# A bidirectional attention and mLSTM layer on 8 cores: the softmax denominators made by one 512-column product, their reciprocal taken over 512 columns in four pieces

## What is computed

```
def one_block(qi):
    s = jnp.einsum('bqkgd,bskd->bkgqs', qi, k) * scale
    p = jax.nn.softmax(s, axis=-1)
    return jnp.einsum('bkgqs,bskd->bqkgd', p, v)
...
attn_out = blocked_gqa_attention(aq, ak, av).astype(x.dtype) * jax.nn.silu(az)
```

## Time and profile before

| | before |
|---|---|
| median of 3 runs | 4118.76 us (4115.62 to 4427.08) |
| the profiled execution | 4113.87 us |
| its span, slowest core | 4112.4 us (4103.0 to 4112.4 over the cores) |
| TensorE (PE) busy | 3939.7 us, 96% |
| weight load (PEld) busy | 2071.8 us, 50% |
| VectorE (DVE) busy | 1964.6 us, 48% |
| ScalarE (ACT) busy | 1723.5 us, 42% |
| GpSimd (POOL) busy | 865.8 us, 21% |
| mean granted TensorE clock | 0.992 to 0.994 of full speed |

### The profile page before, as it was taken

How to read it: one execution, slowest core, us unless ns; L and a number is a source line. 1 busy time by engine, 2 the same in 40 slices (tenths; PEclk the granted TensorE clock), 3 DMA queues, 4 the chain that set the end, 5 groups by cost and what they waited for, 6 DMA issues and landing times.

```text
span 4112.4 us, 73108 instructions; the slowest of 8 cores (4103.0 to 4112.4 us)
## 1 busy us (share of the span) xinstructions
PE 3939.7 (96%) x24102; PEld 2071.8 (50%) x24102; DVE 1964.6 (48%) x4961; ACT 1723.5 (42%) x3691; POOL 865.8 (21%) x1121
## 2 busy tenths in 40 slices
...
GB/s 218 82 86 58 75 46 39 177 131 101 88 53 218 220 111 27 24 37 36 41 94 118 93 47 31 217 220 113 24 29 37 36 21 22 42 36 28 73 181 157
DMA packets 137394, 358.41 MB, mean 87 GB/s; under 512 B 15040, under 2 KB 64576, under 8 KB 122432
## 3 DMA queue, kind: packets, MB, share of 16 engines
...
## 4 chain that ended last, share of the span: by engine, by line
PE 86%; DMA 4%; issue 3%; DVE 3%; ACT 3%; POOL 1%; SPq 0%; DVEq 0%; ACTq 0%; POOLq 0%
PE PP L1189 16%; PE PP L1095 15%; PE PP L681 10%; PE PP L763 8%; PE PP L725 8%; PE PP L776 7%; PE PP L989 6%; PE PP L948 6%; PE PP L801 2%; DMA xnd<-arena 2%; DMA arena<-c_rope 1%; PE PP L1059 1%; PE PP L1062 1%; ACT arena L462 1%; PE PP L468 1%
## 5 line engine op out<-in xcount | busy, mean ns | idle before, releaser
L770 ACT ACTIVATE arena<-PP 128x1024 bf16<-128x1024 f32 x768 | 770.6, 1026 | 153.7 <-PE PP L763 152.4
L1095 PE MATMUL PP<-WR,hT 128*128 128x512 bf16 x3072 | 696.2, 379 | 0.3
L1189 PE MATMUL PP<-WR,mixT 128*128 128x512 bf16 x3072 | 669.4, 379 | 0.0
L681 PE MATMUL PP<-WR,hT 128*128 128x512 bf16 (+1 forms) x3072 | 570.0, 327 | 11.8 <-DMA WR<-w_A 10.6
L1189 PEld LDWEIGHTS PP<-WR,mixT 128*128 128x128 bf16 x3072 | 298.9, 98 | 352.8
L763 PE MATMUL PP<-mixT 128*128 128x512 bf16 x1536 | 458.4, 380 | 7.5 <-ACT arena L770 6.4
L1095 PEld LDWEIGHTS PP<-WR,hT 128*128 128x128 bf16 x3072 | 298.7, 98 | 320.4 <-issue 0.8
L776 PE MATMUL PP<-arena,mixT 128*128 128x512 bf16 x1536 | 457.6, 380 | 2.4 <-ACT arena L770 2.4
L725 PE MATMUL PP<-hT,WR 128*128 128x512 bf16 x1536 | 408.8, 381 | 33.8 <-DMA WR<-w_Z 21.0
L681 PEld LDWEIGHTS PP<-WR,hT 128*128 128x128 bf16 x3072 | 297.4, 98 | 244.8 <-issue 16.5
L659 POOL TENSOR_TENSOR mixT<-arena 128x384 f32<-128x384 f32 (+1 forms) x192 | 196.3, 1023 | 914.2 <-DVE arena L640 882.2
...
## 6 DMA issues: line engine op xcount, KB each, us to landing
arena<-x SPq DMA_DIRECT2D x192, 256.0 KB, 3.3
y<-arena SPq DMA_DIRECT2D x192, 256.0 KB, 3.5
...
arena<-c_rope SPq DMA_DIRECT2D x192, 128.0 KB, 2.0
...
```

The lines of the kernel that those rows point to most:

```text
L681: S.group('pe', [(lambda kc=kc: P.matmul(pv[:, 0:ncol], hT[:, kc, T * 128:(T + 1) * 128], W[:, kc, c0:c0 + ncol], start=(kc == 0), stop=(k ...
L770: S.op('act', lambda: A.activation(PT[t % NPT].ap, spair[t % 2][:, 0:1024], AF.Exp, scale=128.0 ** -0.5), reads=spn[t % 2], writes=[PT[t % ...
L1095: S.group('pe', [(lambda kc=kc: P.matmul(bank(b), hT[:, kc, csl(c)], W[:, kc, 0:512], start=(kc == 0), stop=(kc == KC - 1))) for kc in ran ...
L1189: S.group('pe', [(lambda kc=kc: P.matmul(bank(b), mixT[:, kc, csl(T)], W[:, kc, 0:512], start=(kc == 0), stop=(kc == KC - 1))) for kc in r ...
```

## The change

The two products with different weights and the splitting between them go. One product of 512 columns with a 128x128 weight (`bsum`) adds the partial sums and spreads the result over all 128 partitions. The reciprocal is then taken of all 512 columns, in four instructions of 128 columns put down 1000 ns apart on the virtual clock, and `b5free` comes 100 ns after the last of them. The multiplication reads the reciprocal from SBUF instead of bank 5. The filler's shares are made for 58 steps instead of 56 (passes 1 and 2; the first pass of a sequence keeps 56.0 at its second place, pass 3 keeps 62.0), and in the very first pass of all one gate projection stands one group later.

```
-    b[:, 416:448] = 2.0 * (i[:, None] % 32 < 2)
-    for j in range(4):
-        b[32 * j:32 * j + 2, 480 + 128 * j:608 + 128 * j] = 1.0
+    b[:, 480:608] = 2.0 * (i[:, None] % 32 < 2)
...
-        rec = carve('ar', 30720, [128, 128], F32)
-        rhi = carve('ar', 31232, [128, 128], BF16)
-        rhl = carve('ar', 31488, [128, 128], BF16)
+        rec = carve('ar', 30720, [128, 512], F32)
...
-                    elif n in (1, 5):
+                    elif n in (1, 6):
...
                 def e2():
-                    S.group('pe', [(lambda q=q: P.matmul(bank(5)[32 * q:32 * q + 32, 0:128], sel32,
-                                                         shl.ap[:, 128 * q:128 * (q + 1)], start=True, stop=True,
-                                                         tile_position=(0, 32 * q))) for q in range(4)],
-                            reads=[shl, 'const'], writes=['B5'])
-                    F.now += 120
-
-                def e3():
-                    S.op('dve', lambda: V.reciprocal(rec.ap, bank(5)[:, 0:128]), reads=['B5'], writes=[rec])
-                    S.op('dve', lambda: V.tensor_copy(rhi.ap, rec.ap), reads=[rec], writes=[rhi])
-                    S.op('dve', lambda: V.scalar_tensor_tensor(rhl.ap, rhi.ap, modd, rec.ap, ALU.mult, ALU.add),
-                         reads=[rhi, rec, 'const'], writes=[rhl])
-
-                def e4():
-                    S.group('pe', [(lambda q=q: P.matmul(bank(5)[:, 128 * q:128 * (q + 1)], bcj[q], rhl.ap,
-                                                         start=True, stop=True)) for q in range(4)],
-                            reads=[rhl, 'const'], writes=['B5'])
-                    F.now += 300
+                    S.op('pe', lambda: P.matmul(bank(5), bsum, shl.ap, start=True, stop=True), reads=[shl, 'const'], writes=['B5'])
+                    F.now += T512
+
+                def e3(q):
+                    S.op('dve', lambda: V.reciprocal(rec.ap[:, 128 * q:128 * q + 128], bank(5)[:, 128 * q:128 * q + 128]),
+                         reads=['B5'], writes=[rec])
 
                 def e5():
-                    S.op('dve', lambda: V.tensor_tensor(ott.ap, ott.ap, bank(5), ALU.mult), reads=[ott, 'B5'], writes=[ott])
-                    F.after(1000, b5free)
+                    S.op('dve', lambda: V.tensor_tensor(ott.ap, ott.ap, rec.ap, ALU.mult), reads=[ott, rec], writes=[ott])
...
-                F.chain((150, e0), (300, e1), (2000, e2), (350, e3), (1800, e4), (500, e5), (900, e6))
+                F.chain((150, e0), (300, e1), (1800, e2), (350, lambda: e3(0)), (1000, lambda: e3(1)), (1000, lambda: e3(2)),
+                        (1000, lambda: e3(3)), (100, b5free), (600, e5), (700, e6))
...
-                    rate = total / (62.0 if p == 3 else 56.0)
+                    rate = total / (62.0 if p == 3 else 58.0)
```

3 lines of the change are left out of this document (1 added, 2 removed).

## The result

The changed kernel takes 4158.8 us (median; 4153.6 to 4162.7 in its undisturbed executions) where the kernel before takes 4118.8. The ratio is 1.0096 with an interval of 1.0076 to 1.0116: about 40 us, or 1%, slower.

What follows compares the result with a forecast made beforehand. The attention was taken to run at TensorE's pace, with VectorE about half free. TensorE's saving -24, bank wait +42, ends of passes +10 and weights +1 gave +29 us: median 4148 us, range 4102 to 4174.

Steps and rivals of the forecast that it cites:

- bank wait: Transposes behind a block's sums wait for the last reciprocal to free bank 5: +42 us; as rival 1, 60%.
- What TensorE saves: One product replaces tiled addition and spreading product on TensorE: 0.28 us less per block, 24 us over 87 blocks.
- Ends of passes: Last transposes of passes 0, 1 and 2 come 1.0, 1.8 and 0.7 us later: +10 us over three sequences.
- The spread: Filling work over 58 steps releases the weights later; sequence 1's pass 2 waits longer for w_A: +1 us.
- Hidden: VectorE's added 220 us, the SBUF multiplication and GpSimd's L844 cost nothing; bank 6 in pass 3 not counted.
- Signs: L693 idle some 0.7 us, released by L820 (mean 957 ns); pass 3 2 us shorter, pass 0 3, pass 1 6 longer.
- Rival 2: Transposes come late enough by themselves, so only TensorE's saving and the ends of passes count: 4102 us, 18%.
- Rival 4: Waits of 1.9 us a block nearly everywhere at the transposes: above 4201 us, 4%.
- Rival 3: VectorE's queue delays L640, squares and exponentials; scores wait 0.5 us in 48 blocks, 24 us on top: 4172 us, 18%.

Runs made afterwards that it cites:

- products changed over: Changed kernel with GpSimd multiplying the output with the gate during the reciprocals and VectorE multiplying with the reciprocals last: 4141.9 us, 1.0044.
- later flag: Changed kernel with both multiplications changed over and the flag letting transposes into bank 5 given 2.4 us later in planner's time: 4128.9 us, 1.0028.

## Why the prediction was right, and where not

The forecast was +29 us with the bank wait as its likeliest cause; +40 came, inside the range, and the largest part of it from that cause. That the sum came so near is in part luck: the bank term was some 16 us too large, and terms that it had put at nothing (pass 3, scores behind exponentials, the clock), with 7 us outside the passes that stay unexplained, made up for it and more. By its steps:

- **What TensorE saves: right.** By starts, the median over the 96 blocks is 0.265 us for the tiled addition and 0.223 for the spreading product, and 0.216 for the one product: 0.27 us a block for the forecast 0.28, 26 us in all. (The run with one reciprocal and the kernel before with the same spread differ by 1557.0 - 1526.4 = 30.6 us in the passes, but 8.4 us of that are shorter ends of passes, 8.7 us lost for 17.1.)
- **The bank wait: right mechanism, term too large.** Forecast 42 us; the blocks lost 29.4 us, 3.1 of which were there before. One step that failed is "0.49 us, less the gap that they fill, 0.4": L663 and L668 cost 0.14 us (4.92 against 4.78). In pass 0 of sequences 2 and 3 this halves the wait, 0.38 for 0.7 us, and makes 2.0 us a pass of 4.0. In passes 1 and 2 L635 and L657 between the reciprocals also cost less than put down, 0.2 to 0.8 us, and 28 us became 23. The largest miss is pass 0 of sequence 1, 2.1 us for 6.5: on TensorE's way to the transpose scores waited 0.3 to 1.1 us for exponentials in five of its six blocks, which the prediction had named as a bound and left out of the sum.
- **Ends of passes: the sum right, one term wrong.** 18.1 us were lost before the last transposes and 8.3 before, plus 9.8 for plus 10. Pass 0 came as forecast, 4.77 us from the product for 4.79. In pass 1 the norm starts 8.93 us after the sums, where the forecast had 3.6 + 5.4 = 9.0; what failed is "the transpose 2.55 us after that". It took 3.48, because GpSimd now makes the gate's product (1.26 us) ahead of L671; with the products changed over, the end is 11.36 us instead of 12.41. And the norm's place behind the multiplication, which I held for the cause, is worth only 0.6 us: with one reciprocal it is 11.80, held by the squares of the projection behind the sums.
- **The spread: left nearly out.** It stood in the sum with 1 us for the weights and inside the ends of passes; by itself it costs the kernel before 18 us (1.0044), and taken out of the changed kernel it gives back some 7 to 9. Besides the ends, the scores wait for exponentials: 6.4 us before, 11.8 in the kernel before at 58, 13.2 with one reciprocal, 16.3 in the changed kernel. For w_A there was no loss at all: the wait in sequence 1 went from 10.6 to 6.2 us.
- **Hidden: wrong twice.** "At worst 0.5 us in three blocks, not counted" stood for bank 6 in pass 3. The wait behind L728 grew by 5.0 us, with a smaller one behind L571 that grew from 2.3 to 4.2, together 7 us, and pass 3 gained nothing instead of 2 us a sequence. And GpSimd's idle time before L844 was read as cover for it. The cover that counted was that of the tanh behind it, 1.5 us between 4.9 and 6.4, and the four reciprocals used it up: GpSimd's product now ends at 7.18 and the tanh starts at 7.33. That cost little as long as the bank wait held TensorE too, and showed when this was removed.
- **The clock: not in the sum.** In the twelve passes the granted clock was 1.2 GHz for 18.8 us before, 34.1 in the changed kernel and 27.3 with one reciprocal (medians over the eight cores). Half of such time is lost where TensorE has work throughout: by that, an estimate, up to 8 of the 36 us.
- **Signs.** L820's mean is 956 ns and pass 1 of sequence 2 was 7.3 us longer for some 6; pass 0 was 1.3 us longer for some 3, and pass 3 not shorter.
- **Rivals.** Rival 2 fell: L693 waits 26.0 us for L820. Rival 4 fell with the time. Rival 3 was wrong in the link that I gave, the squares' wait for VectorE went from 180.2 to 173.3 us; scores behind exponentials do grow, by the spread and by the gate's buffer. Its other part, the multiplication from two SBUF tiles: the one in the rows above ran 0.89 us, with GpSimd reading SBUF from 1585.84 for 0.61 us, where the undisturbed one took 0.69. The Trainium skill (SBUF — State Buffer, "Who interferes with whom") calls the port pair that the two engines share an exclusive lock, and the rows agree: the multiplication grew by 0.20 us where 0.34 us of GpSimd's instruction were left at its start, by 0.40 for 0.54 (spread 56) and by 0.80 for 0.95 (one reciprocal), each time by what was left less 0.15. Before the change it read PSUM and one SBUF tile and took 0.69 us beside GpSimd too. In the changed kernel only 13 of 96 ran above 0.8 us.

Step by step the passes go by +13.7 us (spread), -30.6 (the products, with one reciprocal) and +52.5 (three more reciprocals a block), together +35.6; this sum holds by construction, and the steps would be others in another order. Of the 52.5, the blocks' transposes are 29.2, the ends of passes 9.4 (18.1 lost before their transposes in the changed kernel, 8.7 with one reciprocal), pass 3's projections 7, the scores 3. Some 4 us aren't assigned; the 6.8 us more at 1.2 GHz would make up to 3 of them.

## What to carry to other kernels

When an operation is moved from a busy engine to one that is half idle, its load counts for little and its length for much: write down everything that waits for its result or its buffer, with the time each has left, and follow each to the bound engine. Here there were three such followers (bank 5, the gate's buffer, bank 6), two of them each late by less than 1 us in a block of pass 0, so that removing one showed a gain of 0.4 or 0.2 us and both 2.1. A change of a planner's rate that comes along with such an edit should be timed alone, on both sides; here it cost 18 us in the kernel before and some 7 to 9 in the changed one. And an operation that does not need the late result (the gate's multiplication) belongs ahead of it.

## What the runs showed of the chip

- A reciprocal of 128x128 float32 takes 956 ns from PSUM and 950 ns from SBUF. Reading SBUF does not make it cheaper; the copy (691 ns for 128x512) pays only by the bank that it frees.
- Two small VectorE instructions (0.10 and 0.42 us) between two that depend on each other lengthened the chain by 0.14 us, since they fill the 0.10 us gap and overlap with their neighbours.
- A VectorE multiplication of two SBUF tiles that starts while a GpSimd instruction reads SBUF was lengthened by what was left of that instruction less 0.15 us: 0.20 for 0.34, 0.40 for 0.54, 0.80 for 0.95.
- A wait of 3.33 us on TensorE was followed by matmuls at half clock for 3.4 to 6.8 us: pairs of 1.06 us instead of 0.59. In the other three windows of that sequence, ahead of which no such wait stands, the granted clock is 1.00. It does not fall each time: of the 16 ends of pass 1 in sequences 2 and 3 (eight cores) 14 show it behind 3.33 us, 11 behind 3.08 (kernel before, spread 58) 11 behind 2.72 (one reciprocal), 7 and 12 behind 2.28 (products changed over, without and with the later flag), none behind 1.86 (spread 56) or 1.25 (before). The Trainium skill (TensorE: Matmul & The Clock Gate, "What's actually happening") has the idle engine fall to 1.2 GHz; by that the rows agree.
